# Ten residual subtractions of the dense stage on GpSimd instead of VectorE

## The chip, the cores and the metric

One core of one Trainium2 chip. The metric is the device time of one execution in microseconds, the median of three runs.

## The reference

A two-layer backbone for 256 latent tokens of width 1024 with 256 context tokens. Layer 0 mixes tokens by latent attention and pooling and has a dense channel mixer; layer 1 mixes by a 2-D Fourier transform and has a top-2-of-8 expert mixer. Each sublayer is modulated by adaLN rows (shift, scale, gate) that are products of a conditioning vector with `ada_w`. The change is in the dense channel mixer of layer 0:

```python
def swiglu(h, w1, w3, w2):
    return (jax.nn.silu(h @ w1) * (h @ w3)) @ w2

x = x + g2 * swiglu(h, ffn_w1[0], ffn_w3[0], ffn_w2[0])   # 1024 -> 2816 -> 1024, fp32
```

## The kernel before

Everything is fp32. In the dense stage a product is made in three: each operand is split into a high part (the value rounded to the type fp32r) and a low part (the value less its high part), and TensorE adds high x high, high x low and low x high.

**The pieces.** The three weight matrices are cut into 33 pieces of 128 x 2048 numbers (1 MB), in the order of the list `DENSE`: w1 of group 0, w3 of group 0, then for each group g from 1 to 10 w1 of g, w3 of g, w2 of g - 1, and last w2 of group 10. So pieces 4, 7, 10, ..., 31 and 32 are w2, the down projection. Two pieces are one unit (2 MB), which a DMA of the SP queue brings into one of three slots of the tile `ring`.

**Work per piece q.** ScalarE makes the high part (L859) once TensorE is done with piece q - 2, since there are two buffers of high and low parts. VectorE makes the low part (L1043, function `dense_low`, semaphore `low_ready`). TensorE makes 48 products of 128x256: 16 high x high, 16 high x low, and in its third part 16 low x high, in front of which it waits for the low part. w1 and w3 are at L2000, w2 at L1990, the last piece at L1972.

**What else VectorE does in the stage, all in the order of its program.** In iteration q: where piece q - 2 is a w3, the product for the hidden tile (L1317, one operand in PSUM); the low part of piece q; after an odd q the signal `unit_free` that the unit's slot is free; where there was a hidden product, its low part (L1328); and `add_half(q - 2)`, four steps over half an adaLN unit of `ada_w` (L1056 once or not at all, else L1058: a row block times a number, plus the running total, all in SBUF), each waiting for the one before. In four iterations a turn of the finished sums follows (L1101 to L1103). TensorE makes short sum-up products for these (L1649) behind pieces 6, 14, 22 and 30.

**SP's queue** sends unit n once the slot of unit n - 3 is signalled free, and behind it two adaLN halves, each once the half before it in its slot is used up.

```python
                if q:
                    dense_low(q)
                if q % 2 or q == len(DENSE) - 1:
                    u = first_unit[f"ffn{q // 2}"]
                    dve.wait_ge(low_ready, q + 1)
                    dve.sem_inc(unit_free[unit_slot(u)], 1)
```

**GpSimd** clears a few tiles, packs some attention weights and does the pooling windows; its program ends there.

Of the kernel before, what the change touches and what calls it, by code (L numbers as in the profile page):

```python
# [11 lines left out]
ALU = mybir.AluOpType  # L12
# [43 lines left out]
SPLITS_DENSE = 2  # L56
# [45 lines left out]
DENSE = dense_pieces()  # L102
# [18 lines left out]
        (1, 0, 1, 0, True), (1, 1, 1, 1, False), (1, 0, 2, 2, False), (1, 1, 2, 3, True))  # L121
DOWN_ENDS = (1, 4, 6, 7, 8, 9, 10, 11)
DENSE_UNITS = -(-len(DENSE) // 2)

SUMMED = ((0, 10), (0, 11)) + tuple((1, u) for u in range(12))
SUM_GROUPS = ((0, 2), (2, 6), (6, 10), (10, 14))
# [66 lines left out]
def build(nc, vec_d, con_d, rope_d, x_d, ctx_d, ada_d, mixa_d, mixb_d, attn_d, mixout_d, ffn_d,  # L193
          dft_d, fnet_d, router_d, moe_d, out_d):
    ctx = ExitStack()
    with ctx:
# [3 lines left out]
        def sem(name):  # L200
            return ctx.enter_context(nc.semaphore(name))
# [22 lines left out]
        bank = [ctx.enter_context(nc.psum_tensor(f"bank{b}", [P, 512], F32)) for b in range(8)]  # L224
# [11 lines left out]
        def C(name):  # L236
            return con[:, CON[name][0]:CON[name][1]]
# [78 lines left out]
        def plain(ap):  # L316

            return ap.bitcast(F32)
# [41 lines left out]
        four_ready, four_high, four_low = sem("four_ready"), sem("four_high"), sem("four_low")  # L360
        bias_ready, bias_taken = sem("bias_ready"), sem("bias_taken")
        logits_ready, logits_taken, logits_turned = sem("logits_ready"), sem("logits_taken"), sem("logits_turned")
        tok_ready, tok_taken, counts_ready = sem("tok_ready"), sem("tok_taken"), sem("counts_ready")
        gap_ready, odds_ready, mask_ready, rank_ready, loops_ready = (
            sem("gap_ready"), sem("odds_ready"), sem("mask_ready"), sem("rank_ready"), sem("loops_ready"))
        gathered, x_first, x_second = sem("gathered"), sem("x_first"), sem("x_second")
        group_picked, tok_low = sem("group_picked"), sem("tok_low")
        e_used, e_gate, e_hidden, e_turned = sem("e_used"), sem("e_gate"), sem("e_hidden"), sem("e_turned")
# [12 lines left out]
        units, first_unit = [], {}  # L381
# [26 lines left out]
        def unit_slot(n):  # L408
            return n % UNIT_SLOTS
# [5 lines left out]
        def rows_of(run):  # L415

            return ada_rows[:, 0:P * len(RUNS[run][1])]

        def piece_view(n):

            u = first_unit[f"ffn{n // 2}"]
            return view(ring, unit_slot(u) * UNIT + (n % 2) * PIECE, PIECE)
# [231 lines left out]
        @block.gpsimd  # L654
        def _(pool):
            n_step = [0]

            def link(ins):
                n_step[0] += 1
                ins.then_inc(pool_step, 1)  # L660
                pool.wait_ge(pool_step, n_step[0])

            nc.gpsimd.memset(ada_rows, 0.0).then_inc(rows_zero, 1)
            nc.gpsimd.memset(condp[:, :], 0.0).then_inc(rows_zero, 1)
            nc.gpsimd.memset(pool0[:, :, 0:PAD], 0.0).then_inc(pads_zero, 1)
            nc.gpsimd.memset(pool0[:, :, PAD + T:], 0.0).then_inc(pads_zero, 1)

            pool.wait_ge(attn_in, 2 * 16)
            wide, turned = view(work, 0, 2 * HEADS, QK), view(moe, 1536, 2 * HEADS, ROPE)
            nc.gpsimd.tensor_copy(view(moe, 1024, 2 * HEADS, ROPE), wide[:, :, NOPE:]).then_inc(uq_packed, 1)  # L670
            for n in range(2):
                lo, to = 8 * n, 8 * (1 - n)
                for b in (0, 16):
                    nc.gpsimd.tensor_copy(turned[:, :, b + to:b + to + 8], wide[:, :, NOPE + b + lo:NOPE + b + lo + 8]).then_inc(uq_packed, 1)
            nc.gpsimd.tensor_copy(view(moe, 0, 2 * HEADS, NOPE), wide[:, :, 0:NOPE]).then_inc(uq_packed, 1)

            pool.wait_ge(pads_zero, 2)
            pool.wait_ge(rows_zero, 2)
            pool.wait_ge(mixa_taken, 2)
            pool.wait_ge(mixer_low, len(MIXER["mixin"]))  # L680
            pool.wait_ge(con_in, 16)
            n2, n4, n8, n16 = PADDED - 1, PADDED - 3, PADDED - 7, PADDED - 15
            link(nc.gpsimd.tensor_tensor(pool1[:, :, 0:n2], pool0[:, :, 0:n2], pool0[:, :, 1:1 + n2], ALU.add))
            link(nc.gpsimd.tensor_tensor(pool2[:, 1:, 0:n4], pool1[:, 1:, 0:n4], pool1[:, 1:, 2:2 + n4], ALU.add))
            link(nc.gpsimd.tensor_tensor(pool1[:, 2:, 0:n8], pool2[:, 2:, 0:n8], pool2[:, 2:, 4:4 + n8], ALU.add))
            link(nc.gpsimd.tensor_tensor(pool2[:, 3:, 0:n16], pool1[:, 3:, 0:n16], pool1[:, 3:, 8:8 + n16], ALU.add))
            for g, w in enumerate(WINDOWS):
                at = (pool1 if g % 2 == 0 else pool2)[:, g, PAD - w // 2:PAD - w // 2 + T]
                link(nc.gpsimd.tensor_scalar(at, at, 1.0 / w, None, ALU.mult))
                for n, ends in enumerate((at[:, 0:PAD], at[:, T - PAD:T])):  # L690
                    fix = C("edge")[:, (2 * g + n) * PAD:(2 * g + n + 1) * PAD]
                    link(nc.gpsimd.tensor_tensor(ends, ends, fix, ALU.mult))
                rows = pool0[:, g, PAD:PAD + T]
                nc.gpsimd.tensor_tensor(rows, at, rows, ALU.subtract).then_inc(pooled, 1)


        @block.scalar
# [284 lines left out]
        def _(dve):  # L982
# [325 lines left out]
            for q in range(len(DENSE)):  # L1308
                coming = q - SPLITS_DENSE
                if coming >= 0 and DENSE[coming][0] == "w3":  # L1310
                    g = DENSE[coming][1]
                    dve.wait_ge(gate_ready, g + 1)
                    dve.wait_ge(used, coming + 1)
                    if g >= 1:
                        dve.wait_ge(hidden_high, g)
                        dve.wait_ge(hidden_low, g)
                    nc.vector.tensor_tensor(hidden_tmp, gate_tmp[:, g % 2],  # L1317
                                            bank[1][:, :].rearrange("p (a b) -> p a b", a=2),
                                            ALU.mult).then_inc(hidden_ready, 1)
                if q:  # L1320
                    dense_low(q)
                if q % 2 or q == len(DENSE) - 1:
                    u = first_unit[f"ffn{q // 2}"]
                    dve.wait_ge(low_ready, q + 1)
                    dve.sem_inc(unit_free[unit_slot(u)], 1)
                if coming >= 0 and DENSE[coming][0] == "w3":
                    dve.wait_ge(hidden_high, g + 1)
                    nc.vector.tensor_tensor(hidden_parts[g % 2][:, 1], hidden_tmp, plain(hidden_parts[g % 2][:, 0]),  # L1328
                                            ALU.subtract).then_inc(hidden_low, 1)
                if 0 <= q - HALF_LAG < HALVES:  # L1330
                    add_half(q - HALF_LAG)
                if q in (9, 17, 25, 32):
                    take_sums((9, 17, 25, 32).index(q))
# [107 lines left out]
                                               op0=ALU.mult, op1=ALU.subtract).then_inc(tok_low, 1)  # L1441

            token_low(0)
            dve.wait_ge(rank_ready, 1)
            link(nc.vector.scalar_tensor_tensor(out=rank, in0=bank[5][:, 0:16].rearrange("p (a b) -> p a b", a=2),
                                                scalar=1.0, in1=mask, op0=ALU.add, op1=ALU.mult))
            full, more = cols(200, 1), cols(201, MAX_ROUNDS - 1)
# [17 lines left out]
            def gates():  # L1465
# [8 lines left out]
                link(nc.vector.tensor_tensor(best, best, key, ALU.add))  # L1474
                link(nc.vector.tensor_copy(table(gate_at), best.unsqueeze(2).to_broadcast(by_round)))

                dve.wait_ge(counts_ready, 1)
                link(nc.vector.tensor_reduce(full, bank[4][:, 0:8], AX_X, ALU.max))
                for r in range(1, MAX_ROUNDS):
                    link(nc.vector.tensor_scalar(cols(200 + r, 1), full, CAP * r + 0.5, None, ALU.is_gt))  # L1480
# [121 lines left out]
        def _(pe):  # L1602
# [353 lines left out]
            for q, (kind, g) in enumerate(DENSE):  # L1956
# [6 lines left out]
                elif g >= 1:  # L1963
                    pe.wait_ge(gate_ready if kind == "w1" else hidden_ready, g)
                if q == len(DENSE) - 1:
                    pe.wait_ge(low_ready, q + 1)
                    for pair in range(4):
                        for n, (w, right) in enumerate(((high, 0), (high, 1), (low, 0))):
                            w = w.rearrange("p (a b) -> p a b", a=2)
                            for j in range(2):  # L1970
                                for k in (2 * pair, 2 * pair + 1):
                                    last = mm(bank[FFN_BANKS[pair]][:, (k % 2) * T:(k % 2) * T + T], w[:, j, k * P:(k + 1) * P],  # L1972
                                              hidden_parts[g % 2][:, right, j, :], start=False,
                                              stop=(n == 2 and j == 1), skip_group_check=True)
                        last.then_inc(ffn_ready, 1)
                        if pair == 2:
                            pe.wait_ge(ada_taken, NRUNS + len(SUM_GROUPS))
                            quarters(2, 2 + KD)
                    continue
                parts = ((high, 0), (low, 0), (high, 1)) if q == 0 else ((high, 0), (high, 1), (low, 0))  # L1980
                for n, (w, right) in enumerate(parts):
                    if q < 2 and n == 0:
                        continue
                    if n == (1 if q == 0 else 2):
                        pe.wait_ge(low_ready, q + 1)
                    if kind == "w2":
                        w = w.rearrange("p (a b) -> p a b", a=2)
                        for j in range(2):
# [117 lines left out]
            pe.wait_ge(mask_ready, 1)  # L2106
            mask, all0, all1 = small[:, 184:200], small[:, 224:232], small[:, 232:240]
            mm(bank[5][:, 0:16], C("before"), mask, start=True, stop=False)
            mm(bank[5][:, 8:16], C("mean"), all0, start=False, stop=True).then_inc(rank_ready, 1)
            mm(bank[4][:, 0:8], C("mean"), all0, start=True, stop=False)  # L2110
            mm(bank[4][:, 0:8], C("mean"), all1, start=False, stop=True).then_inc(counts_ready, 1)

            def gather(group):

# [181 lines left out]
```

## Time and profile before

| | |
|---|---|
| median of three runs | 1308.31 us (1308.15 to 1309.08) |
| profiled execution, its own time | 1307.7 us |
| its span, first to last instruction | 1305.9 us |
| TensorE (PE) busy | 1286.7 us, 99% |
| VectorE (DVE) busy | 435.8 us, 33% |
| ScalarE (ACT) busy | 225.9 us, 17% |
| GpSimd (POOL) busy | 17.4 us, 1% |
| dense stage in the span | about 144 to 344 us |
| expert stage | from 401 us on |

The span lacks 1.8 us of the execution's time, which lie around it. The shares are averages over stages that differ much: VectorE's third of the span is nearly all of the dense stage and little of the expert stage. PE is TensorE's matmuls, PEld its weight loads, SP the queue that sends the transfers.

### The profile page before, as it was taken

The numbers are of one execution on the slowest core, as the hardware profiler recorded it, in microseconds if no ns is written. First come the engines' busy times: TensorE is split into PE (matmuls) and PEld (weight loads), VectorE is DVE, ScalarE is ACT, GpSimd is POOL, SyncE is SP. The second block draws the span as 40 slices with busy tenths as digits, with TensorE's granted clock in tenths as the row PEclk, the third lists the DMA queues.
The fourth block names the chain that finished last, engine by engine and source line by source line (L and its number), as shares of the span: only waits on it lengthen the run. The fifth ranks groups of instructions, "written<-read, shape, count | busy, mean of one in ns | idle before, by whom it ended". The sixth has DMA issues, their size and how long they took to land.

```text
span 1305.9 us, 28074 instructions
## 1 busy us (share of the span) xinstructions
PE 1286.7 (99%) x12465; PEld 665.3 (51%) x12465; DVE 435.8 (33%) x866; ACT 225.9 (17%) x384; POOL 17.4 (1%) x34
## 2 busy tenths in 40 slices
PE   9999999999999999999999999999999999999997
PEld 7857999999994333333333333533333333333333
DVE  5488699999753010210120020111102002011203
ACT  5274543333442000000000000000000000000002
POOL 0400000000000000000000000000000000000000
PEclk9999999999999999999999999999999999999999
DMA  9953699997566879999999999999899999999980
GB/s 389 360 215 130 262 371 345 380 370 272 218 248 243 361 304 411 420 390 401 422 421 368 412 420 375 405 402 392 336 411 421 377 402 421 415 377 412 420 351 34
DMA packets 60691, 459.68 MB, mean 352 GB/s; under 512 B 6944, under 2 KB 7200, under 8 KB 9248
## 3 DMA queue, kind: packets, MB, share of 16 engines
q1 hardware_dynamic: 60576, 457.92, 86.7%
q8 instruction: 99, 1.62, 0.5%
q14 instruction: 16, 0.13, 0.0%
HBM read 456.78 MB, written 1.11 MB: 351 GB/s over the span
## 4 chain that ended last, share of the span: by engine, by line
PE 81%; DVE 11%; DMA 4%; ACT 2%; issue 2%; DVEq 0%; SPq 0%; ACTq 0%
PE bank L2155 44%; PE bank L2168 22%; DVE work L1058 5%; PE bank L1729 4%; DMA ring<-in_ada 3%; DVE split L1043 3%; PE bank L1780 2%; PE bank L2135 1%; PE bank L2125 1%; PE bank L1621 1%; DMA ring<-in_mixout 1%; PE bank L1915 1%; PE bank L2000 0%; PE bank L1990 0%; PE bank L1972 0%
## 5 line engine op out<-in xcount | busy, mean ns | idle before, releaser
L2155 PE MATMUL bank<-ring,work 128*32 128x512 f32 (+1 forms) x6144 | 584.9, 539 | 1.1 <-DVE moe L1553 1.1
L2155 PEld LDWEIGHTS bank<-ring,work 128*32 128x32 f32 x6144 | 199.2, 110 | 377.3 <-issue 344.2
L2168 PE MATMUL bank<-ring,moe 128*32 128x512 f32 x2688 | 294.1, 592 | 0.0
L1553 DVE TENSOR_TENSOR moe<-moe,bank 128x256 f32<-128x256 f32 (+1 forms) x96 | 31.5, 384 | 658.4 <-ACT moe L954 658.4
L2168 PEld LDWEIGHTS bank<-ring,moe 128*32 128x32 f32 x2688 | 87.4, 110 | 197.6 <-issue 196.3
L954 ACT ACTIVATE moe<-bank 128x256 f32<-128x256 f32 (+1 forms) x96 | 27.4, 357 | 792.3 <-PE bank L2155 792.3
L2000 PE MATMUL bank<-split 128*128 128x256 f32 x1024 | 125.7, 284 | 2.6 <-DVE split L1043 2.6
L2000 PEld LDWEIGHTS bank<-split 128*128 128x128 f32 x1024 | 123.8, 192 | 3.6 <-DVE split L1043 3.3
L1043 DVE TENSOR_TENSOR split<-ring,split 128x2048 fp32r<-128x2048 f32 x33 | 75.5, 2290 | 6.3 <-ACT split L859 3.0
L1058 DVE SCALAR_TENSOR_TENSOR work<-ring,condp,work 128x512 f32<-128x512 f32 x98 | 73.7, 752 | 6.2 <-DMA ring<-in_ada 2.3
L859 ACT ACTIVATE split<-ring 128x2048 fp32r<-128x2048 f32 x31 | 59.3, 1914 | 71.4 <-PE bank L2000 70.4
L1990 PE MATMUL bank<-split 128*128 128x256 f32 x480 | 59.4, 283 | 0.0
L1990 PEld LDWEIGHTS bank<-split 128*128 128x128 f32 x480 | 58.3, 192 | 0.4 <-issue 0.4
L1729 PE MATMUL bank<-split 128*128 128x256 f32 x384 | 47.5, 284 | 0.0
L1729 PEld LDWEIGHTS bank<-split 128*128 128x128 f32 x384 | 46.4, 192 | 1.4 <-issue 1.4
L1539 DVE SCALAR_TENSOR_TENSOR xT<-bank,ada,xT 128x256 f32<-128x256 f32 x64 | 25.9, 476 | 62.0 <-PE bank L2135 62.0
L1557 DVE STREAM_TRANSPOSE moe<-moe 128x256 f32<-128x256 f32 (+1 forms) x96 | 31.7, 381 | 0.0
L998 DVE TENSOR_TENSOR split<-ring,split 128x1024 fp32r<-128x1024 f32 (+1 forms) x24 | 28.0, 1183 | 7.8 <-ACT split L719 7.5
L719 ACT ACTIVATE split<-ring 128x1024 fp32r<-128x1024 f32 (+1 forms) x24 | 24.1, 1018 | 33.1 <-PE bank L1729 18.9
L1780 PE MATMUL bank<-split 128*128 128x256 f32 x168 | 24.8, 303 | 0.0
L1531 DVE SCALAR_TENSOR_TENSOR split<-bank,small,split 128x512 fp32r<-128x512 f32 x16 | 11.3, 747 | 36.9 <-ACT split L944 36.9
L1780 PEld LDWEIGHTS bank<-split 128*128 128x128 f32 x168 | 21.4, 191 | 2.1 <-issue 1.6
(256 smaller groups left out, 624.7 us busy)
## 6 DMA issues: line engine op xcount, KB each, us to landing
ring<-in_moe SPq DMA_DIRECT2D x336, 1024.0 KB, 13.6
ring<-in_ffn SPq DMA_DIRECT2D x16, 2048.0 KB, 8.9
ring<-in_ada SPq DMA_DIRECT2D x28, 1024.0 KB, 7.3
ring<-in_ada SPq DMA_DIRECT2D x10, 2048.0 KB, 9.6
ring<-in_mixout SPq DMA_DIRECT2D x2, 2048.0 KB, 8.7
ring<-in_fnet SPq DMA_DIRECT2D x2, 2048.0 KB, 9.0
ring<-in_mixa SPq DMA_DIRECT2D x2, 1024.0 KB, 17.5
tail<-tables SPq DMA_DIRECT2D x8, 256.0 KB, 18.0
```

Of the source, the lines that this page charges most:

```text
L859: nc.scalar.activation(high_d[:, q % SPLITS_DENSE, :], piece_view(q), ACT.Copy).then_inc(high_ready, 1)
L998: nc.vector.tensor_tensor(mixer_part(m, 1), mixer_source(m), plain(mixer_part(m, 0)), ALU.subtract).then_inc(mixer_low, 1)
L1043: nc.vector.tensor_tensor(low_d[:, q % SPLITS_DENSE, :], piece_view(q), plain(high_d[:, q % SPLITS_DENSE, :]), ALU.subtract).then_inc(low_ ...
L1058: ins = nc.vector.scalar_tensor_tensor(out=total, in0=half_view(h)[:, k, :], scalar=weight, in1=total, op0=ALU.mult, op1=ALU.add)
L1553: nc.vector.tensor_tensor(gate_e[:, g, 0:n], gate_e[:, g, 0:n], bank[g][:, n:2 * n], ALU.mult).then_inc(e_hidden, 1)
L1557: nc.vector.transpose(hiddenT[phase % 2][:, g, 0:n], gate_e[:, g, 0:n]).then_inc(e_turned, 1)
L1729: last = mm(bank[banks[c // 2]][:, (c % 2) * T:(c % 2) * T + T], parts[left][:, k, j * P:(j + 1) * P], source[right][:, k0 + k, :], start= ...
L1780: last = mm(out, parts[left][:, k, lo:hi], h_in[right][:, k0 + k, 0:n], start=((left, right) == PRODUCTS[0] and k0 + k == 0 and opens), st ...
L1990: last = mm(bank[FFN_BANKS[k // 2]][:, (k % 2) * T:(k % 2) * T + T], w[:, j, k * P:(k + 1) * P], hidden_parts[g % 2][:, right, j, :], star ...
L2000: last = mm(bank[kind == "w3"][:, j * T:(j + 1) * T], w[:, k, j * P:(j + 1) * P], h_parts[:, right, k, :], start=(n == 0 and j == 0 and k ...
L2155: last = mm(bank[g][c * QUAD:(c + 1) * QUAD, 0:count * P], x_group[:, 4 * half + k, j * CAP + g * QUAD:j * CAP + (g + 1) * QUAD], source[: ...
L2168: last = mm(bank[3 + n][c * QUAD:(c + 1) * QUAD, :], hiddenT[phase % 2][:, g, blk * QUAD:(blk + 1) * QUAD], source[:, j, n * 512:(n + 1) * ...
```

## The change

The low parts of ten w2 pieces (4, 7, ..., 31; the list `POOL_LOWS`; the last piece stays) are made by GpSimd, behind its other work, with a semaphore `pool_low` of their own. The helper `low_done(eng, q)` waits for the low part of piece q on whichever of the two semaphores counts it. A unit's slot is signalled free by the engine that makes the low part of its second piece, after it has waited for both. Two semaphores of the expert routing, `rank_ready` and `counts_ready`, become one with two counts, `ranks_ready`.

```diff
+POOL_LOWS = [q for q, (kind, _) in enumerate(DENSE[:-1]) if kind == "w2"]
...
+        def low_done(eng, q):
+
+            if q in POOL_LOWS:
+                eng.wait_ge(pool_low, POOL_LOWS.index(q) + 1)
+            else:
+                eng.wait_ge(low_ready, q + 1 - sum(n < q for n in POOL_LOWS))
...
+            for q in POOL_LOWS:
+                pool.wait_ge(high_ready, q + 1)
+                nc.gpsimd.tensor_tensor(low_d[:, q % SPLITS_DENSE, :], piece_view(q), plain(high_d[:, q % SPLITS_DENSE, :]),
+                                        ALU.subtract).then_inc(pool_low, 1)
+                if q % 2:
+                    low_done(pool, q)
+                    low_done(pool, q - 1)
+                    pool.sem_inc(unit_free[unit_slot(first_unit[f"ffn{q // 2}"])], 1)
...
-                if q:
+                if q and q not in POOL_LOWS:
                     dense_low(q)
-                if q % 2 or q == len(DENSE) - 1:
+                if q not in POOL_LOWS and (q % 2 or q == len(DENSE) - 1):
                     u = first_unit[f"ffn{q // 2}"]
-                    dve.wait_ge(low_ready, q + 1)
+                    low_done(dve, q)
+                    if q % 2:
+                        low_done(dve, q - 1)
                     dve.sem_inc(unit_free[unit_slot(u)], 1)
...
                 if q == len(DENSE) - 1:
-                    pe.wait_ge(low_ready, q + 1)
+                    low_done(pe, q)
...
                     if n == (1 if q == 0 else 2):
-                        pe.wait_ge(low_ready, q + 1)
+                        low_done(pe, q)
```

## Rows read from the trace of the kernel before

**Rows 1.** The page, busy times: engine, us, share of the span, instructions

```profile
PE 1286.7 (99%) x12465; PEld 665.3 (51%) x12465; DVE 435.8 (33%) x866; ACT 225.9 (17%) x384; POOL 17.4 (1%) x34
```

**Rows 2.** Windows: stretch, busy time of PE, PEld, DVE, ACT, POOL, clock, DMA

```profile
149.25:337.55 188.30, 185.66 (x1619) 183.72 (x1617) 173.64 (x184) 72.30 (x55) 0.00 (x0) 1.00 0.91 350
...
401.00:1305.00 904.00, 895.33 (x9032) 312.10 (x9030) 119.26 (x355) 46.34 (x129) 0.00 (x0) 1.00 0.92 376
```

**Rows 3.** Waits of PE, 149 to 346 us: total, times, longest

```profile
PE bank L2000 <- DVE split L1043: 2.6, 2, 1.9
```

**Rows 4.** Timeline of PE, dense stage: start, us, line, shapes, count, wait

```profile
168.45 5.92 PE L1990 MATMUL bank<-split 128*128 128x256 f32 x48
...
245.29 9.76 PE L2000 MATMUL bank<-split 128*128 128x256 f32 x80
256.90 2.17 PE L2000 MATMUL bank<-split 128*128 128x256 f32 x16 [1.85 <-DVE split L1043]
...
305.19 7.94 PE L2000 MATMUL bank<-split 128*128 128x256 f32 x64 [0.71 <-DVE split L1043]
...
318.73 12.02 PE L2000 MATMUL bank<-split 128*128 128x256 f32 x96
330.68 1.08 PE L1649 MATMUL bank<-work,con 128*32 128x128 f32 x32
```

**Rows 5.** Timeline of DVE, one group of three pieces

```profile
248.68 0.69 DVE L1328 TENSOR_TENSOR split<-ring,split 128x512 fp32r<-128x512 f32 x1
249.29 3.11 DVE L1058 SCALAR_TENSOR_TENSOR work<-ring,condp,work 128x512 f32<-128x512 f32 x4
...
254.55 2.29 DVE L1043 TENSOR_TENSOR split<-ring,split 128x2048 fp32r<-128x2048 f32 x1
256.76 0.48 DVE L1056 TENSOR_SCALAR work<-ring,condp 128x512 f32<-128x512 f32 x1
...
259.64 2.29 DVE L1043 TENSOR_TENSOR split<-ring,split 128x2048 fp32r<-128x2048 f32 x1
262.08 3.11 DVE L1058 SCALAR_TENSOR_TENSOR work<-ring,condp,work 128x512 f32<-128x512 f32 x4
265.52 0.69 DVE L1317 TENSOR_TENSOR ring<-ring,bank 128x512 f32<-128x512 f32 x1 [0.33 <-DVE work L1058]
```

**Rows 6.** Timeline of DVE: low part of piece 3, and of pieces 30 and 31

```profile
160.99 2.28 DVE L1043 TENSOR_TENSOR split<-ring,split 128x2048 fp32r<-128x2048 f32 x1
...
326.22 4.49 DVE L1043 TENSOR_TENSOR split<-ring,split 128x2048 fp32r<-128x2048 f32 x2
```

**Rows 7.** Waits of DVE, 150 to 338 us

```profile
DVE work L1058 <- DMA ring<-in_ada: 2.3, 2, 1.7
```

**Rows 8.** Timeline of ACT: high part of piece 19

```profile
251.25 1.91 ACT L859 ACTIVATE split<-ring 128x2048 fp32r<-128x2048 f32 x1 [2.44 <-PE bank L2000]
```

**Rows 9.** Lines of POOL, by form: count, busy us, mean ns

```profile
L692 POOL TENSOR_TENSOR ring<-ring,con 128x8 f32<-128x8 f32 x8 | 1.6, 202 | 0.6
...
L683 POOL TENSOR_TENSOR ring<-ring 128x1084 f32<-128x1084 f32 x1 | 2.0, 1990 | 0.0
...
L686 POOL TENSOR_TENSOR ring<-ring 128x257 f32<-128x257 f32 x1 | 0.7, 739 | 0.1
```

**Rows 10.** DVE and POOL at 46.3 us, and their likes (min/median/max ns)

```profile
34.32 0.95 DVE L998 TENSOR_TENSOR split<-ring,split 128x768 fp32r<-128x768 f32 x1
...
46.33 1.09 DVE L998 TENSOR_TENSOR split<-ring,split 128x768 fp32r<-128x768 f32 x1
...
46.56 1.02 POOL L674 COPY moe<-work 128x128 f32<-128x128 f32 x1
...
L674 POOL COPY moe<-work x4: 297/298/1024, 45.9 to 46.6; 128x128 f32<-128x128 f32 x4
```

**Rows 11.** SP's timeline, and the page's transfers: KB each, us to landing

```profile
262.02 0.33 SPq L541 DMA_DIRECT2D ring<-in_ffn  x1
...
ring<-in_ffn SPq DMA_DIRECT2D x16, 2048.0 KB, 8.9
```

More of the change, by code:

```diff
@@ L362, in build @@
         logits_ready, logits_taken, logits_turned = sem("logits_ready"), sem("logits_taken"), sem("logits_turned")
-        tok_ready, tok_taken, counts_ready = sem("tok_ready"), sem("tok_taken"), sem("counts_ready")
-        gap_ready, odds_ready, mask_ready, rank_ready, loops_ready = (
-            sem("gap_ready"), sem("odds_ready"), sem("mask_ready"), sem("rank_ready"), sem("loops_ready"))
+        tok_ready, tok_taken, pool_low = sem("tok_ready"), sem("tok_taken"), sem("pool_low")
+        gap_ready, odds_ready, mask_ready, ranks_ready, loops_ready = (
+            sem("gap_ready"), sem("odds_ready"), sem("mask_ready"), sem("ranks_ready"), sem("loops_ready"))
         gathered, x_first, x_second = sem("gathered"), sem("x_first"), sem("x_second")
@@ L1443, in _ @@
             token_low(0)
-            dve.wait_ge(rank_ready, 1)
+            dve.wait_ge(ranks_ready, 1)
             link(nc.vector.scalar_tensor_tensor(out=rank, in0=bank[5][:, 0:16].rearrange("p (a b) -> p a b", a=2),
@@ L1475, in gates @@
                 link(nc.vector.tensor_copy(table(gate_at), best.unsqueeze(2).to_broadcast(by_round)))
-                dve.wait_ge(counts_ready, 1)
+                dve.wait_ge(ranks_ready, 2)
                 link(nc.vector.tensor_reduce(full, bank[4][:, 0:8], AX_X, ALU.max))
@@ L2108, in _ @@
             mm(bank[5][:, 0:16], C("before"), mask, start=True, stop=False)
-            mm(bank[5][:, 8:16], C("mean"), all0, start=False, stop=True).then_inc(rank_ready, 1)
+            mm(bank[5][:, 8:16], C("mean"), all0, start=False, stop=True).then_inc(ranks_ready, 1)
             mm(bank[4][:, 0:8], C("mean"), all0, start=True, stop=False)
-            mm(bank[4][:, 0:8], C("mean"), all1, start=False, stop=True).then_inc(counts_ready, 1)
+            mm(bank[4][:, 0:8], C("mean"), all1, start=False, stop=True).then_inc(ranks_ready, 1)
             def gather(group):
```

## The prediction

> **What bounds the kernel now.** I read the page's busy times first: TensorE is busy 99% of the span and VectorE 33% [rows 1], but the change touches one stage only, the dense channel mixer. So I took the windows view of that stage, from the first product that waits for a low part (149.25 us) to the start of the last piece (337.55 us), and of the expert stage behind it [rows 2]. In the dense stage VectorE is busy 173.6 of 188.3 us, as good as all of it, beside a TensorE that is busy 185.7; the clock is 1.00. GpSimd does nothing there. Behind 401 us TensorE is busy 895 of 904 us at the full clock and waits for nothing that the dense stage makes: the whole program behind the dense stage moves with its end, microsecond for microsecond.
>
> Next, TensorE's own waits between 149 and 346 us: one kind, low parts of VectorE's L1043, 2.6 us in two waits [rows 3]. TensorE's timeline shows them, 1.85 us at 255 and 0.71 us at 305 [rows 4]; the row at 318.73 takes 12.02 us for 96 products, where 80 products in 9.76 us make some 0.12 each and 0.16 for the tail, so 11.7: another 0.3 us is lost in it, when VectorE's low part of piece 30 ends at about 328.5 [rows 6] and TensorE wanted it at 328.35. Together 2.9 us: that is all that a faster VectorE could give.
>
> Third, VectorE's timeline over one group of three pieces (17: w1, 18: w3, 19: w2) [rows 5]. Between one hidden product (L1317, at 245.65) and the next (265.52) come low 17, the hidden low, four adaLN steps, from 252.4 to 254.5 a turn of sums, low 18, four steps, low 19, four steps, each starting as the one before it ends. The reader is to see that low 18 ends at 256.84 and TensorE resumes at 256.90, while low 19 ends at 261.93 and TensorE wants it only 3.84 us (32 of 48 products) into the next piece, at 262.75. VectorE is the pacemaker by a hair: a group costs TensorE 48 x 3 x 0.12 = 17.3 us and a share of the short sum-ups (1.08 us or less, four in all [rows 4]), 17.6; from low 3 at 160.99 to low 30 at 326.22 VectorE needs 165.2 us for nine groups, 18.4 each, of which 2.3 us in all are waits for adaLN rows in flight [rows 6, 7].
>
> **The change part by part.** Ten subtractions of 128x2048 (pieces 4, 7, ..., 31) leave VectorE. Each takes 2.29 us there; from its start to the next instruction's it is 2.2 us (254.55 to 256.76), or 2.4 where the slot's signal follows it (259.64 to 262.08) [rows 5], 2.3 on average. Nine lie in the stretch 160.99 to 326.22, the tenth behind it. They go to GpSimd.
>
> Price on GpSimd: no such row exists. A sum of two SBUF inputs over 1084 columns takes 1.990 us, one over 8 columns 0.202 [rows 9]: 1.66 ns a column, so 2048 columns give 0.202 + 2040 x 1.66 ns = 3.6 us. The dearest row for its size is 257 columns in 0.739 us: 2.16 ns a column, 4.6 us for 2048. I take 3.6, from the row nearest in size, and keep 4.6 as the upper end; for the lower, without the fixed 0.2 us, 3.4. The Trainium skill (GPSIMD Engine Reference, 3.1 Elementwise — side-by-side cycle accounting) lists 4497 ns for this very size; the 1084-column row here is cheaper than that figure scaled to its size (2.4 us), and by the page's figure the forecast below would be 8 us later, at 1325.7.
>
> If the two engines ran side by side, this would be free: the high part of a w2 piece is there about 2 us after the piece before it starts (high 19 is started at 251.25 and takes 1.91 [rows 8]), and its low is wanted 5.76 + 3.84 = 9.6 us after that start. GpSimd would be done at 2 + 3.6 = 5.6, four us early.
>
> But they don't seem to. The one place where this trace has GpSimd reading SBUF beside a VectorE instruction with two SBUF inputs is at 46.3 us [rows 10]: the L998 subtraction of 768 columns, 0.95 us elsewhere, takes 1.09, and the GpSimd copy of 128 columns issued at 46.56, whose three likes take 0.30, takes 1.02 and ends just behind the subtraction (47.42 against 47.58). One waits for the other to end. And in the dense stage nearly everything on VectorE has two SBUF inputs: the lows (L1043), the adaLN steps (L1058, the half's rows and the running total), the hidden low (L1328). The Trainium skill says the same (SBUF — State Buffer, Who interferes with whom): a VectorE instruction with two SBUF inputs and a GpSimd instruction that reads SBUF exclude each other for the whole instruction. The rows at 46.3 us agree, with 0.72 us lost on one side and 0.14 on the other.
>
> So a low part moved to GpSimd still takes VectorE's time, and more of it: 3.6 + 0.1 for the two handovers (an estimate from the 0.14 us above) instead of 2.3, 1.4 us more per piece. Only L1317 and the sum turns (an input in PSUM, or a single one) run beside it. The sum over the stretch that ends with low 30: nine pieces x 1.4 = +12.6; the waits for adaLN rows, 2.3, vanish, since a slower VectorE gives the transfers more time; about 1.0 us of sum turns and hidden products falls beside a GpSimd instruction: +12.6 - 2.3 - 1.0 = **+9.3 us**. Low 30 ends 9.3 us later, and TensorE was already waiting for it, so the stage's end moves by as much. The 3 us by which low 3 is early (it ends at 163.3; piece 4 starts at 168.45 [rows 4], so piece 3's third part at 166.5) are already used up in the trace of before, where low 18 is late, so they don't lower the sum. The tenth piece: its high part is there before low 30 ends, GpSimd takes 3.6 us behind low 30, TensorE wants it 1.9 + 1.0 + 3.8 = 6.7 us behind low 30: hidden by TensorE's own work; bare, it would cost 3.6.
>
> What stalls instead: GpSimd will mostly be let in around the low part of the w3 piece before, so low(w3) and, behind it, the adaLN steps, the hidden product and low(w1) on VectorE are late, and TensorE waits for L1043 in the third parts, up to 3 to 4 us at a time, about 12 us in all (2.9 + 9.3).
>
> The slot signals: five units (ending with pieces 7, 13, 19, 25, 31) are freed by GpSimd, the rest by VectorE. SP sent the next transfer at 262.02, right behind low 19 [rows 11]; such a transfer takes 8.9 us to land, and the slot is read again three pieces later, 17.3 us. A signal late by a few us costs nothing; bare, it would cost as much as it is late over 8. Behind SP's wait stand the adaLN halves, which VectorE, now the late one, won't wait for. Merging the semaphores of ranks and counts costs nothing: both are raised by TensorE in the same order as before. GpSimd has no other work from here to the end [rows 2].
>
> The sum is made against the profiled execution: 1307.7 + 9.3 = 1317.0. The median of before lies 0.6 above that execution: **1317.6 us**, slower by 0.7%. About 0.2% (2.6 us) is what a measurement of this kernel can tell from no change.
>
> **The rivals.** (a) *No exclusion that counts*: the two engines mix finely or VectorE's steps don't collide with GpSimd's. VectorE then needs 18.4 - 2.3 = 16.1 us a group against TensorE's 17.6, all low parts are in time, the 2.9 us go: 1308.3 - 2.9 = 1305.4. The point from which it decides: a moved piece that costs VectorE under 2.3 us turns the sign, and under 17.6 - 16.1 = 1.5 us all of the 2.9 is gained. For it: a single collision is the whole evidence, and it was with another GpSimd instruction, of one input. Against it: the copy lost 0.72 us there. 0.14. (b) *Exclusion, but GpSimd goes in VectorE's holes*: VectorE keeps the turn while its instructions follow one another within 0.03 us, and GpSimd gets it where VectorE waits for TensorE or runs L1317 or a sum turn. Per group TensorE's 17.6 less VectorE's 16.1 leaves 1.5, with L1317 (0.7) 2.2 of the 3.6 needed: 1.4 short x 9 = 12.6, less VectorE's lead of 3.2 at the start and the 2.9 of stalls and 2.3 of waits of before: +4.2, 1312.5. For it: the copy did wait for the whole subtraction. 0.10. (c) *Exclusion in part*: GpSimd shuts VectorE out for two thirds of its time, 2.4 us, so that the piece costs 2.3 + 0.2: 9 x 0.2 less 1 to 2.3 us of overlap and waits, 1308 to 1309. 0.06. (d) *My forecast*, exclusion with VectorE losing GpSimd's time: 0.70; its own range is set by the price: 3.4 gives 1315.8, with another 2 us of overlap 1313.8; 4.6 gives 1326.6.
>
> **Numbers.** The range from 1309 to 1329 holds (d) and (b) and leaves out (a), half of (c) and a little at the top, some 2 in 10. Faster by over 0.2%: most of (a), 0.11. Within 0.2%: the rest of (a) and (c), 0.09. Slower: (d) and (b), 0.80.
>
> **What would show it.** Right: GpSimd's subtraction rows at 3.6 us or, where they waited, longer; L1058 or L1043 rows of VectorE that take up to 3.6 us more than their 0.75 and 2.29; about 12 us of TensorE waits for L1043 in the dense stage, and the w2 lows themselves never waited for; the stage behind unchanged. Wrong: L1058 at a steady 0.75 while GpSimd subtracts, which would be rival (a); GpSimd rows of 6 us and more with VectorE's unchanged, rival (b).

## The result and the profile after

The changed kernel takes **1324.6 us** (median, 1323.3 to 1325.1), the kernel before 1308.2 us (1308.0 to 1309.1): a ratio of 1.0122, with a 95% interval of 1.0110 to 1.0134. Slower by 16.4 us; forecast were 1317.6 us and a range of 1309 to 1329. The profiled execution took 1324.5 us, 16.8 more than that of before.

The page's busy times, and VectorE, GpSimd and the clock in 40 slices:

```profile
PE 1290.8 (98%) x12465; PEld 668.4 (51%) x12465; DVE 444.9 (34%) x856; ACT 225.6 (17%) x384; POOL 71.6 (5%) x44
...
DVE  5488799899774110111120020112002002011203
...
POOL 0400033213100000000000000000000000000000
PEclk9999999989999999999999999999999999999999
```

Against [rows 1] VectorE has ten instructions less and is busy 9 us *more*. Ten subtractions of 2.29 us left it, so some 32 us have come from somewhere. The groups by line and shape say where (count, busy us, mean ns, idle before). First two of VectorE's in the kernel before, between 150 and 338 us:

```profile
L1058 DVE SCALAR_TENSOR_TENSOR work<-ring,condp,work 128x512 f32<-128x512 f32 x98 | 73.7, 752 | 6.2 <-DMA ring<-in_ada 2.3
...
L1056 DVE TENSOR_SCALAR work<-ring,condp 128x512 f32<-128x512 f32 x14 | 6.7, 481 | 0.0
```

In the changed kernel GpSimd's, then VectorE's between 149 and 355 us:

```profile
L706 POOL TENSOR_TENSOR split<-ring,split 128x2048 fp32r<-128x2048 f32 x10 | 54.3, 5426 | 230.1 <-ACT split L876 230.1
```

```profile
L1075 DVE SCALAR_TENSOR_TENSOR work<-ring,condp,work 128x512 f32<-128x512 f32 x98 | 93.2, 951 | 10.0 <-DMA ring<-in_ada 6.7 <-DVE split L1060 0.2
L1060 DVE TENSOR_TENSOR split<-ring,split 128x2048 fp32r<-128x2048 f32 x22 | 50.4, 2291 | 4.0 <-ACT split L876 3.2
L1073 DVE TENSOR_SCALAR work<-ring,condp 128x512 f32<-128x512 f32 x14 | 15.5, 1108 | 1.0 <-DVE work L1075 0.7
L1347 DVE TENSOR_TENSOR split<-ring,split 128x512 fp32r<-128x512 f32 x11 | 7.6, 690 | 1.2 <-DVE split L1060 1.1
L1334 DVE TENSOR_TENSOR ring<-ring,bank 128x512 f32<-128x512 f32 x11 | 7.6, 687 | 3.8 <-PE bank L2019 2.3 <-DVE work L1075 0.9 <-DVE ada L1120 0.3
L1120 DVE TENSOR_TENSOR ada<-small,vec 128x16 f32<-128x16 f32 x3 | 3.7, 1227 | 0.1
```

The same 98 adaLN steps (L1058 before, now L1075) took 73.7 us and take 93.2; the 14 first steps (L1056, now L1073) took 6.7 and take 15.5; one addition of 16 columns (L1120) takes 3.3 us instead of 0.2. That is 19.5 + 8.8 + 3.1 = 31.4 us by which VectorE's instructions are stretched. Its 22 low parts (L1060) keep their 2291 ns: where the two meet, GpSimd waits for the low part to end and the instruction behind it is the one held. The timelines side by side show it at three collisions, VectorE's first:

```profile
181.35 2.29 DVE L1060 TENSOR_TENSOR split<-ring,split 128x2048 fp32r<-128x2048 f32 x1
183.56 4.85 DVE L1073 TENSOR_SCALAR work<-ring,condp 128x512 f32<-128x512 f32 x1
...
247.54 3.12 DVE L1075 SCALAR_TENSOR_TENSOR work<-ring,condp,work 128x512 f32<-128x512 f32 x4 [4.64 <-DMA ring<-in_ada]
...
261.44 0.69 DVE L1119 TENSOR_REDUCE small<-work 128x16 f32<-128x512 f32 x1
262.16 3.33 DVE L1120 TENSOR_TENSOR ada<-small,vec 128x16 f32<-128x16 f32 x1
```

```profile
182.13 5.99 POOL L706 TENSOR_TENSOR split<-ring,split 128x2048 fp32r<-128x2048 f32 x1 [12.08 <-ACT split L876]
...
241.52 5.86 POOL L706 TENSOR_TENSOR split<-ring,split 128x2048 fp32r<-128x2048 f32 x1 [13.31 <-ACT split L876]
260.92 4.54 POOL L706 TENSOR_TENSOR split<-ring,split 128x2048 fp32r<-128x2048 f32 x1 [13.54 <-ACT split L876]
```

At 182.13 GpSimd waits for VectorE's low part to end (183.6), runs to 188.1, and the 0.48 us step behind it takes 4.85. The one at 260.92 starts beside a transpose and a reduction, which it doesn't hold up, and is clean: 4.54 us; the small addition behind them, with two SBUF inputs, is held until GpSimd ends. At 241.5 it runs in a hole, while VectorE waits for adaLN rows, and costs nothing.

TensorE's waits in the stage, and its timeline where they cost most:

```profile
PE bank L2019 <- DVE split L1060: 13.6, 8, 5.5
PE bank L1696 <- ACT ring L860: 1.4, 1, 1.4
```

```profile
217.45 9.34 PE L2019 MATMUL bank<-split 128*128 128x256 f32 x64 [2.72 <-DVE split L1060]
...
268.19 3.78 PE L2019 MATMUL bank<-split 128*128 128x256 f32 x16 [5.47 <-DVE split L1060]
```

2.6 us [rows 3] have become 13.6, all for VectorE's own low parts and none for GpSimd's. Behind the two longest waits the products are slow as well: 64 in 9.34 us, where 64 took 7.94 [rows 4], and 16 in 3.78, where 16 took 2.17. The windows around them have the mean clock at 0.92 and 0.87 of full speed, and the 16 products alone at 0.50, which is the level of 1.2 GHz instead of 2.4:

```profile
204.97:226.62 21.65, 18.93 (x146) 18.73 (x145) 20.61 (x20) 6.75 (x5) 5.88 (x2) 0.92 0.92 347
...
246.23:271.77 25.54, 19.36 (x146) 18.95 (x145) 22.90 (x26) 6.75 (x5) 5.69 (x2) 0.87 0.86 359
...
268.19:271.77 3.58, 3.58 (x16) 3.58 (x17) 3.40 (x6) 0.00 (x0) 0.00 (x0) 0.50 0.08 34
```

### The profile page after: what moved, and what is told of

Read it like the earlier page. It is cut to its first block, busy times and chain, and to the rows that moved or that the text cites. A ratio compares the mean times of both kernels' runs of the same rounds, so it can differ in the third digit from the quotient of the medians.

```text
span 1322.7 us, 28074 instructions
## 1 busy us (share of the span) xinstructions
PE 1290.8 (98%) x12465; PEld 668.4 (51%) x12465; DVE 444.9 (34%) x856; ACT 225.6 (17%) x384; POOL 71.6 (5%) x44
## 4 chain that ended last, share of the span: by engine, by line
PE 79%; DVE 13%; DMA 4%; ACT 2%; issue 1%; POOL 0%; DVEq 0%; SPq 0%; ACTq 0%; POOLq 0%
PE bank L2174 44%; PE bank L2187 22%; DVE work L1075 6%; PE bank L1748 4%; DMA ring<-in_ada 3%; DVE split L1060 2%; PE bank L1799 1%; PE bank L2154 1%; DVE work L1073 1%; PE bank L2144 1%; PE bank L1640 1%; DMA ring<-in_mixout 1%; DMA ring<-in_fnet 1%; DMA ring<-in_ctx 1%; PE bank L1934 1%
## 5 line engine op out<-in xcount | busy, mean ns | idle before, releaser
L2019 PE MATMUL bank<-split 128*128 128x256 f32 x1024 | 129.9, 288 | 13.6 <-DVE split L1060 13.6
L2019 PEld LDWEIGHTS bank<-split 128*128 128x128 f32 x1024 | 127.0, 196 | 15.6 <-DVE split L1060 15.2
L1075 DVE SCALAR_TENSOR_TENSOR work<-ring,condp,work 128x512 f32<-128x512 f32 x98 | 93.2, 951 | 10.0 <-DMA ring<-in_ada 6.7
L706 POOL TENSOR_TENSOR split<-ring,split 128x2048 fp32r<-128x2048 f32 x10 | 54.3, 5426 | 230.1 <-ACT split L876 230.1
L2009 PE MATMUL bank<-split 128*128 128x256 f32 x480 | 59.5, 284 | 0.0
L2009 PEld LDWEIGHTS bank<-split 128*128 128x128 f32 x480 | 58.4, 192 | 0.4 <-issue 0.4
L1060 DVE TENSOR_TENSOR split<-ring,split 128x2048 fp32r<-128x2048 f32 x23 | 52.7, 2291 | 5.7 <-ACT split L876 3.2
L1748 PE MATMUL bank<-split 128*128 128x256 f32 x384 | 47.5, 284 | 0.0
L1748 PEld LDWEIGHTS bank<-split 128*128 128x128 f32 x384 | 46.4, 192 | 1.4 <-issue 1.4
L736 ACT ACTIVATE split<-ring 128x1024 fp32r<-128x1024 f32 (+1 forms) x24 | 24.0, 1018 | 34.0 <-PE bank L1748 18.9
L1799 PE MATMUL bank<-split 128*128 128x256 f32 x168 | 24.8, 303 | 0.0
```

The lines of the kernel that those rows point to most:

```text
L706: nc.gpsimd.tensor_tensor(low_d[:, q % SPLITS_DENSE, :], piece_view(q), plain(high_d[:, q % SPLITS_DENSE, :]), ALU.subtract).then_inc(pool ...
L1060: nc.vector.tensor_tensor(low_d[:, q % SPLITS_DENSE, :], piece_view(q), plain(high_d[:, q % SPLITS_DENSE, :]), ALU.subtract).then_inc(low_ ...
L1075: ins = nc.vector.scalar_tensor_tensor(out=total, in0=half_view(h)[:, k, :], scalar=weight, in1=total, op0=ALU.mult, op1=ALU.add)
L1748: last = mm(bank[banks[c // 2]][:, (c % 2) * T:(c % 2) * T + T], parts[left][:, k, j * P:(j + 1) * P], source[right][:, k0 + k, :], start= ...
L1799: last = mm(out, parts[left][:, k, lo:hi], h_in[right][:, k0 + k, 0:n], start=((left, right) == PRODUCTS[0] and k0 + k == 0 and opens), st ...
L2009: last = mm(bank[FFN_BANKS[k // 2]][:, (k % 2) * T:(k % 2) * T + T], w[:, j, k * P:(k + 1) * P], hidden_parts[g % 2][:, right, j, :], star ...
```

## The experiments

Each was timed beside the kernel before on one chip; ratios are to it. "Changed" at the head of a run means that its edit is made on the changed kernel. The diffs show the edit's core; `...` stands for lines left out.

**GpSimd reads beside an otherwise unchanged kernel.** On the kernel before: nine extra subtractions of 128x2048 on GpSimd into an idle tile, none waited for before the stage ends. Both inputs are the same tile, and the instruction takes 3.6 us (last row below) where the changed kernel's took 4.5.

```diff
+            for q in POOL_LOWS:                      # 4, 7, ..., 28
+                pool.wait_ge(high_ready, q + 1)
+                nc.gpsimd.tensor_tensor(moe[:, 0:PIECE], xT[:, :], xT[:, :], ALU.subtract).then_inc(pool_low, 1)
...
```

> The kernel before, with nine extra GpSimd subtractions of 128x2048 (two SBUF inputs), started at the high parts of pieces 4, 7, ..., 28, whose result nobody uses; VectorE keeps all its low parts. Theory A, the two engines exclude each other while GpSimd reads and VectorE has two SBUF inputs: VectorE loses 3.5 to 4.4 us for each, 31 to 40 us in all, and nothing is taken off it, so 1338 to 1348 us. Rival B, the changed kernel loses its time by hand-overs (low parts or slot signals that come late from GpSimd): nobody waits for GpSimd here, so 1308.3 us, no change.

1334.2 us, ratio 1.0191 (1.0174 to 1.0208): +25 us from work that nobody waits for. The rival, that hand-overs alone carry the loss, is out. It is less than the 31 to 40 forecast. The shorter instruction is one reason; the other is that not all of it fell on work of VectorE: VectorE's stretched rows hold 26.5 us (17.5 in L1065, 6.7 in the one-input steps, 2.3 in the small additions) of nine times 3.6, or 32.4. GpSimd's group and VectorE's steps, and from the timeline one clean row of GpSimd's:

```profile
L699 POOL TENSOR_TENSOR moe<-xT 128x2048 f32<-128x2048 f32 x9 | 39.3, 4362 | 233.6 <-ACT split L866 233.6
...
L1065 DVE SCALAR_TENSOR_TENSOR work<-ring,condp,work 128x512 f32<-128x512 f32 x98 | 91.2, 931 | 5.7 <-DMA ring<-in_ada 1.7
```

```profile
267.05 3.60 POOL L699 TENSOR_TENSOR moe<-xT 128x2048 f32<-128x2048 f32 x1 [15.44 <-ACT split L866]
```

**GpSimd writes but doesn't read.** Changed, with the subtraction replaced by two memsets of the low part's buffer; the ten low parts are left out.

```diff
-                nc.gpsimd.tensor_tensor(low_d[:, q % SPLITS_DENSE, :], piece_view(q), plain(high_d[...]), ALU.subtract)
+                link(nc.gpsimd.memset(plain(low_d[:, q % SPLITS_DENSE, :]), 0.0))
+                nc.gpsimd.memset(plain(low_d[:, q % SPLITS_DENSE, :]), 0.0).then_inc(pool_low, 1)
```

> The changed kernel, with GpSimd's subtraction replaced by two memsets of the low part's buffer (the low parts of ten down-projection pieces are left out, zeros stand in them): about as long on GpSimd (525 ns for 512 columns before, so some 4 us for both), but nothing is read. Theory A, what counts is GpSimd's reading of SBUF: VectorE's rows are no longer stretched and all low parts are in time, 2.9 us under before, 1305.4 us. Rival A2, any GpSimd instruction that uses SBUF shuts VectorE out: about 1315 us. Rival B, hand-overs by GpSimd cost the time: they are all still here, so about 1320 us or more.

1304.5 us, ratio 0.9968 (0.9955 to 0.9980). TensorE waits for no low part at all. GpSimd is busy nearly as long (1.8 us for each memset, 3.7 for a pair, against 4.5), behind the same high parts and with the same signals, so neither its presence nor its hand-overs cost the 16 us. VectorE's steps (columns as above):

```profile
L1075 DVE SCALAR_TENSOR_TENSOR work<-ring,condp,work 128x512 f32<-128x512 f32 x98 | 73.7, 752 | 17.0 <-DMA ring<-in_ada 13.3 <-DVE split L1060 0.5
...
L1073 DVE TENSOR_SCALAR work<-ring,condp 128x512 f32<-128x512 f32 x14 | 9.4, 670 | 1.1 <-DVE work L1075 0.7 <-DMA ring<-in_ada 0.3
```

The two-input steps are at their old 752 ns. The one-input first steps aren't: 670 ns instead of 481. Three of the 14 were held, to 1.05, 1.29 and 1.74 us, each beside a memset.

**GpSimd reads one input.** Changed, with the subtraction replaced by `tensor_copy` of the piece; the ten low parts are left out here too, the buffers hold the whole piece.

> The changed kernel with GpSimd's subtraction replaced by a copy of the piece (one SBUF input, some 1.9 us by the copy of 1024 columns in 1.04 us; the low parts of ten pieces hold the whole piece instead, the values are wrong). Theory A, VectorE is shut out for as long as GpSimd's instruction lasts: 1.9 to 2.0 us lost for 2.3 us saved, so near before, 1305 to 1309 us. Rival B, hand-overs: the hand-overs are the same as in the changed kernel, some 1320 us.

1308.4 us, ratio 1.0005 (0.9995 to 1.0014). Between the two. A copy takes 1.90 us where it doesn't wait, hardly more than a memset's 1.81, and it does stretch the two-input steps: four of them take 4.62 us instead of 3.11. Nearly the same length with and without a read, so it is the reading that holds the two-input steps. In all VectorE's steps lose 7.3 and 3.4 us and its small additions 1.0, 11.7 us for ten copies and not 19 to 20, since some copies fell on waits of VectorE; 20.7 were taken off it. The three runs stand in order, 0, 1.9 and 4.5 us of reading per piece giving 1304.5, 1308.4 and 1324.6 us, but the middle time isn't collisions alone: TensorE's one wait for a low part, 2.8 us, also has a wait of 3.2 us for adaLN rows ahead of it on VectorE.

**Half the pieces.** Changed, with `POOL_LOWS` only 4, 10, 16, 22, 28.

> The changed kernel with only the five even pieces (4, 10, 16, 22, 28) on GpSimd; the odd ones and all slot signals stay with VectorE. Theory A: half the collisions, and the low part of piece 31 and its slot signal are as in before, so +7 us, 1315 us (1313 to 1317). Rival B, the slot signals from GpSimd (only odd pieces have them) carry the loss: 1308 us or under.

1316.8 us, ratio 1.0060 (1.0044 to 1.0077), +8.0. Half the collisions, half the loss, though all slot signals are VectorE's here. VectorE's two-input steps take 92.6 us instead of 73.7, so they lose 18.9 for the 11.5 that left VectorE: 7.4 of the 8.0.

**The signals alone.** On the kernel before: GpSimd frees the slots of the five units, VectorE makes all low parts.

```diff
+            for q in W2_ODD:                         # 7, 13, 19, 25, 31
+                pool.wait_ge(low_ready, q + 1)
+                pool.sem_inc(unit_free[unit_slot(first_unit[f"ffn{q // 2}"])], 1)
...
```

> The kernel before with only the other half of the change: all low parts on VectorE, the slots of the five units that end with a w2 piece signalled free by GpSimd, and the merged semaphore. Theory: the signal is no cost, 1308.3 us within 0.5. Rival B: a part of the 16 us shows, over 1310 us.

1308.6 us, ratio 1.0000 (0.9990 to 1.0009). The signal and the merged semaphore are free.

**The bare price.** On the kernel before: four instructions ahead of GpSimd's work, at 3.6 to 19 us.

```diff
+            link(nc.gpsimd.tensor_tensor(split[:, 6 * PIECE:7 * PIECE], moe[:, 0:PIECE], moe[:, 256:256 + PIECE], ALU.subtract))
+            link(nc.gpsimd.tensor_tensor(moe[:, 0:PIECE], moe[:, 0:PIECE], moe[:, 256:256 + PIECE], ALU.subtract))
+            link(nc.gpsimd.tensor_tensor(moe[:, 0:PIECE], moe[:, 0:PIECE], moe[:, 1:1 + PIECE], ALU.add))
+            link(nc.gpsimd.tensor_tensor(moe[:, 0:1084], moe[:, 0:1084], moe[:, 1024:1024 + 1084], ALU.add))
...
```

> The kernel before, with four GpSimd instructions ahead of its work, at 2 to 20 us where VectorE does next to nothing (their results are used by nobody): 128x2048 subtract of two different column ranges with an fp32r result, the same with an fp32 result, 128x2048 add with the second input one column on, and 128x1084 add with inputs 1024 columns apart. The price read off the rows of before was 3.6 us for 2048 columns; the changed kernel's least row is 4.54. Theory: the price is 4.5 us for both subtractions, and the add with a shift of one column takes 3.6 (the row that I went by had such a shift); the 1084 columns apart then take 2.5, not 2.0. Rival: the bare price is 3.6 everywhere and the rest of 4.54 is collisions.

GpSimd's timeline of that run:

```profile
3.65 4.51 POOL L669 TENSOR_TENSOR split<-moe 128x2048 fp32r<-128x2048 f32 x1
8.25 4.53 POOL L670 TENSOR_TENSOR moe<-moe 128x2048 f32<-128x2048 f32 x1
12.85 3.60 POOL L671 TENSOR_TENSOR moe<-moe 128x2048 f32<-128x2048 f32 x1
16.53 2.55 POOL L672 TENSOR_TENSOR moe<-moe 128x1084 f32<-128x1084 f32 x1
```

As the theory said. The result's type doesn't matter (4.51 and 4.53 us). Where the second input starts one column behind the first (or is the same, above) the instruction takes 3.60 us; 256 columns on it takes 4.5, though the two still overlap in most of their columns, and 1024 columns on it takes 2.55 us for 1084 columns, where the pooling sum of [rows 9], one column on, has 1.99. The last two are both additions, so it isn't the operation. (The kernel itself took 1314.2 us in this run: the added work holds up its start.)

**The tenth piece.** Changed, with piece 31 back on VectorE; run twice, the second time beside the changed kernel.

> The changed kernel with piece 31 back on VectorE. In the changed kernel's trace that piece's low part and slot signal come at 348.1, the fnet transfer behind it starts 2 us later against the rest, and TensorE waits 1.4 us for a square of ScalarE behind the stage. Theory: this wait goes, 1323.2 us, 1.4 under the changed kernel. Rival, the tenth piece is hidden as the prediction had it: 1324.6 us, no difference.

> The changed kernel once more, unaltered, as the yardstick for the three others of this call: 1324.6 us, within 1.

> The changed kernel with piece 31 back on VectorE, once more, now beside the changed kernel on one chip: 1.4 to 2 us under it.

1322.6 us (ratio 1.0104) at first; the second time 1323.4 (1.0111) against 1324.0 (1.0112) for the changed kernel. The wait of 1.4 us at L1696 is gone in both traces; the saving in time came out as 0.6 us beside the changed kernel and as some 2 us between two separate timings, and is too small for these timings to show.

**The transfer in the way.** Changed, without the entry of `EARLY` that sends an expert piece behind unit ffn8.

> The changed kernel, with the one expert piece that SP sends behind unit ffn8 sent behind the dense stage instead. In the changed kernel that 1 MB goes out at 231.25 us in one bunch with a unit (232.88) and an adaLN half (234.03), and VectorE waits 4.64 us for that half. Theory: VectorE's waits for adaLN rows grew from 2.3 to 6.7 us since SP stands behind VectorE's late steps and then sends in bunches; without the extra megabyte the long wait falls by some 2.5 us, and the kernel by up to as much, 1322 to 1324 us. Rival: the wait comes from the slot signals of GpSimd and stays.

1323.9 us (1.0117), beside 1324.0: no difference. The wait did fall, from 6.8 us of adaLN waits in the changed kernel timed beside it to 4.3, and the longest is gone, but the time was not given back. The four steps that had waited 3.9 us then meet GpSimd's instruction, which had run in that hole:

```profile
243.28 7.00 DVE L1075 SCALAR_TENSOR_TENSOR work<-ring,condp,work 128x512 f32<-128x512 f32 x4 [0.39 <-DMA ring<-in_ada]
```

**ScalarE instead of GpSimd.** On the kernel before: ScalarE makes the first adaLN step of each even half, a product of 128x512 with a number per row, at the end of its iteration; VectorE waits for it and adds the other three row blocks.

```diff
+                half = q - HALF_LAG
+                if 0 <= half < HALVES and half % 2 == 0:
+                    u = half // 2
+                    act.wait_ge(half_in[0], 16 * (u + 1))
...
+                    nc.scalar.activation(ada_sum[:, u % SUM_BUFFERS, :], half_view(half)[:, 0, :], ACT.Copy,
+                                         scale=cond[:, 0, 0:1]).then_inc(pool_low, 1)
...
                     if h % 2 == 0 and k == 0:
-                        ins = nc.vector.tensor_scalar(total, half_view(h)[:, k, :], weight, None, ALU.mult)
+                        continue
...
```

> The kernel before, with VectorE relieved by ScalarE instead: the first adaLN step of each even half (14 products of 128x512 with a number, 0.48 us each on VectorE) is done by ScalarE, which is busy 38% of the stage. Theory: VectorE is the pacemaker by a hair, 7 us less work makes all low parts timely, the 2.9 us of stalls go, 1305.4 us (0.2% faster). Rival: ScalarE waits for the half's transfer in order and its high parts come late, 1308 us or more.

**1305.4 us**, ratio 0.9975 (0.9965 to 0.9984), over five rounds: faster than both kernels. TensorE's waits for low parts in the stage, 2.6 us before:

```profile
PE bank L2018 <- DVE split L1059: 0.8, 2, 0.6
```

**Both together.** The last edit on the changed kernel.

> The changed kernel together with the edit that gave 1305.4 us alone (ScalarE makes the first adaLN step of each even half). Theory: VectorE with GpSimd behind it is the one bound of the stage, so 14 steps of 0.5 us off VectorE come off the time in full, and not only 3 us: 6 to 7 us under the changed kernel, 1317 to 1319 us. Rival: most of the loss stands in waits of TensorE that have other causes, and it gains 3 us or less.

1321.2 us (1.0091), 2.9 under the changed kernel's 1324.0 and not 6 to 7: the number is the rival's. The 14 steps are gone from VectorE, and what it saved came back as waits:

```profile
L1083 DVE SCALAR_TENSOR_TENSOR work<-ring,condp,work 128x512 f32<-128x512 f32 x98 | 97.5, 995 | 16.7 <-DMA ring<-in_ada 9.8 <-ACT work L896 3.0 <-DVE split L1068 0.7
```

9.8 us for adaLN rows instead of 6.8, and 3.0 for ScalarE; TensorE, too, waits 1.3 us for a high part of ScalarE, a wait that neither kernel has in the stage. So "VectorE and GpSimd are the one bound of the stage" is too simple. My reading, which no run isolates, is that the loop from a finished half over SP's queue and the transfer to the next half is nearly as tight.

## Why the prediction was right, and where its size was off

*What bounds the kernel.* Right. A VectorE that loses nothing to GpSimd (the memsets) or is relieved by ScalarE gives 4.3 and 3.0 us, and the intervals of both ratios hold the 2.9 us of [rows 3, 4]; and nothing behind the stage takes the loss back: low 30 ends 15.2 us later, the execution 16.8.

*The mechanism.* Right: the collision of [rows 10] was the whole story in small. GpSimd and VectorE take turns, instruction by instruction, when GpSimd reads SBUF and VectorE has two SBUF inputs. The nine extra subtractions show it without any hand-over, the memsets and copies show that it is the reading. One line of the forecast was too narrow: it let only L1317 and the sum turns, "an input in PSUM, or a single one", run beside GpSimd and didn't price the one-input first step (L1056, now L1073). The transpose and the reduction of the sum turn did run on, but the first step was held as long as a two-input one, 4.85 us instead of 0.48, and makes 8.8 of the 31.4 us. The Trainium skill (SBUF — State Buffer, Who interferes with whom) has this rule too, and its other half: a VectorE instruction in a mode that uses both ports, which `tensor_scalar` can enter, contends with GpSimd, there without the condition that GpSimd reads. The memset run agrees, with 670 ns for the first steps instead of 481. Rival (a), no exclusion, is out; rival (b), GpSimd in VectorE's holes, happened in full once by chance (241.5 us) and in part once (201.5 us), not as a rule; rival (c) is out at 4.3 to 4.4 us lost per plain collision (7.36 us instead of 3.11 for four steps at 164.0, 4.85 instead of 0.48 for one at 183.6).

*The sum.* The step that was off is the sum over the stretch from low 3 to low 30: it came out at +9.3, and measured are +15.2 (180.4 us, from 160.96 to 341.38, for 165.2 in [rows 6]). Term by term:

| term | predicted | measured |
|---|---|---|
| nine GpSimd instructions (the forecast with 0.1 each for hand-overs) | 9 x 3.7 = 33.3 | 9 x 4.54 = 40.9 |
| of it beside work or waits of VectorE | -1.0 | -9.5, the difference to the 31.4 of stretched rows |
| nine low parts off VectorE | -20.7 | -20.7 |
| change of the waits for adaLN rows | -2.3 | +4.4 (2.3 to 6.7) |
| sum | +9.3 | +15.1 |

The last measured term is a difference and the other rows add up to 15.1 by it; of the 9.5, 4.5 are the instruction at 241.5 that met a wait, 1.9 the one at 201.5 that met a wait in part, and 1.4 the sum turn at 260.9. No hand-over showed: a plain collision costs VectorE a little less than GpSimd's 4.54 us.

The price was mis-sized by 0.9 us because I took it from the row nearest in size, whose second input lies one column behind the first. The 257-column row that I kept as the upper end was right at 2.16 ns a column. So was the figure of the Trainium skill (GPSIMD Engine Reference, 3.1 Elementwise — side-by-side cycle accounting), 4497 ns, against 4.51 and 4.53 us here; I had set it aside for a cheaper row of another form.

The waits for adaLN rows were to vanish, since a slower VectorE gives the transfers more time. They grew. SP's queue is in order and waits for the same VectorE: a half's transfer goes out once VectorE is done with the half that had its slot. SP's timeline in the changed kernel (start, time over which they were issued):

```profile
221.31 9.90 SPq L605 DMA_DIRECT2D ring<-in_ada  x2
231.25 1.58 SPq L572 DMA_DIRECT2D ring<-in_moe  x1
232.88 0.43 SPq L549 DMA_DIRECT2D ring<-in_ffn  x1
234.03 6.89 SPq L605 DMA_DIRECT2D ring<-in_ada  x2
```

It stands from 221 to 231 us behind the half that the collision at 223.6 us held up, then sends 4 MB in a bunch, and the half sent at 234.03 lands 13.5 us later, at 247.5. That VectorE is slower isn't enough for this: beside the nine extra subtractions it ends later still, and its waits for adaLN rows are 1.7 us. They are long in the runs in which work was taken off VectorE, 6.3 us with ScalarE's help, 10.0 beside the copies, 13.6 beside the memsets; the changed kernel has both, late halves and less work between them. Which of the two makes its 6.7 us was not tested by itself. And this term and the one above it aren't independent: GpSimd's instruction at 241.5 ran for nothing in just that wait, and the run without the expert piece shows that closing the hole only moves the loss. Together the two were -3.3 in the forecast and are -5.1, so the price carries the miss: 7.6 us more, of which these two took back 1.8, and 5.8 were missing from the sum. The forecast's error was thus partly hidden: with 4.54 in it the sum would have been +16.9, about 1325.2 us, close to the 1324.6 measured, but low 30 came only 15.2 later, by an overlap and waits of other sizes, and the rest lies behind it.

*The tenth piece* was to be hidden, and TensorE indeed never waits for low 31. What I didn't follow is its slot signal: GpSimd sends it at 348.1, the fnet unit goes out at 348.24 instead of 15 us behind the 330.80 of before (346), ScalarE waits 2.6 us for it, and TensorE 1.4 us for a square behind that. With piece 31 on VectorE the wait is gone. By the traces 1.4 of the last 1.6 us are this; the timings are too coarse to confirm it.

*What would show it.* Right: stretched L1075 rows (by up to 4.4 us, 3.6 forecast), 13.6 us of waits for VectorE's low parts (12 forecast), none for GpSimd's. Not foreseen: the clock fell twice behind waits of 2.7 and 5.5 us, which made the products some 3 us slower; that this added to the time was not shown, since VectorE waited for no product of TensorE between 205 and 341 us.

## What to carry to other kernels

GpSimd is no spare VectorE: where it read SBUF, the VectorE instruction with two SBUF inputs that came next stood until it was done, and so did the one-input product. A two-input subtraction is twice as long there (4.5 us for 2.29), so the move costs more of VectorE than it frees. Before moving work between engines, look which of their instructions would stand side by side and with what inputs; of what was tried here, only the memset, which reads nothing, left VectorE's two-input steps alone, and what ScalarE can do (a product with a number per row) is better given to ScalarE, which took 7 us off VectorE here and won 3. And where a pacemaker's work is changed, follow the transfers that wait for it before writing that they gain time.

## What the hardware showed that I had not expected

A two-input GpSimd instruction over 2048 fp32 columns takes 4.5 us when its inputs lie in two tiles or 256 columns apart in one, and 3.6 when they are the same or one column apart; with inputs apart, the result's type doesn't matter. Overlap isn't what counts, since 256 columns apart most columns are shared. The kernel's own pooling sums (GpSimd in the kernel before) narrow it down: their inputs lie 1, 2, 4 and 8 columns apart, in this order, [rows 9] having the first and the last:

```profile
L684 POOL TENSOR_TENSOR ring<-ring 128x807 f32<-128x807 f32 x1 | 1.5, 1535 | 0.1
L685 POOL TENSOR_TENSOR ring<-ring 128x530 f32<-128x530 f32 x1 | 1.1, 1077 | 0.1
```

Less the 0.202 us of the 8-column row these are 1.66, 1.67 and 1.68 ns a column up to 4 columns apart and 2.16 at 8, and the 4.5 us for 2048 columns are 2.1. Why is open, and the row at 8 is the only one of its size; no run varied the distance alone.

A memset on GpSimd, which reads nothing, leaves two-input steps of VectorE at 752 ns, yet three of VectorE's one-input products with a number took up to 1.74 us beside it instead of 0.48.

GpSimd was not kept waiting by a busy VectorE: its ten subtractions took 4.54 to 6.53 us, so by the 4.54 none waited longer than 2.0 us, less than one low part of 2.29 us, though VectorE's instructions mostly stood back to back.
